# Modulation sums of a two-block transformer kernel: four row groups side by side on the partitions, and an opening in smaller steps

## What is computed

```python
    c_act = jax.nn.silu(c)                       # (1, 2048)
    for l in range(DEPTH):                       # DEPTH = 2
        shift, scale, gate = jnp.split(c_act @ w_ada[l] + b_ada[l], 3, axis=-1)   # w_ada[l]: 2048 x 6144
        h = rms_norm_2(x, norm_w[l]) * (1.0 + scale[:, None, :]) + shift[:, None, :]
        ...
        x = x + gate[:, None, :] * y
```

## Time and profile before

| | |
|---|---|
| median of three runs | 2554.61 us |
| profiled execution: span from the first to the last instruction | 2553.1 us |
| PE busy | 2513.7 us (98%) |
| DVE busy | 1935.9 us (76%) |
| ACT busy | 1223.6 us (48%) |
| DMA, mean over the span | 202 GB/s |

### The profile page before, as it was taken

One profiled execution on the slowest core, in us unless ns is written; L12 is line 12 of the kernel. 1 busy time (PEld: TensorE's weight loads), 2 busy tenths in 40 slices (PEclk: granted clock), 3 DMA queues, 4 the chain that ended last, 5 costly groups with the idle time before them and its releaser, 6 DMA issues.

```text
span 2553.1 us, 33576 instructions
## 1 busy us (share of the span) xinstructions
PE 2513.7 (98%) x12735; PEld 2109.3 (83%) x12735; DVE 1935.9 (76%) x3285; ACT 1223.6 (48%) x1808; POOL 15.1 (1%) x32
## 2 busy tenths in 40 slices
PE   8999999999999999999999999999999999999999
PEld 6888888888888888878888869888788798888777
DVE  7888988998899888676555647666986667668875
ACT  4444444444444444445555446453455565434553
POOL 0000000000000000000000000000000000000000
PEclk9999999999999999999999999999999999999999
DMA  8787777777787867545445445444445544444444
GB/s 307 257 294 268 277 255 284 280 272 273 247 292 267 299 228 279 202 162 185 142 136 177 157 116 179 150 141 138 143 158 182 176 150 150 134 133 157 153 161 139
DMA packets 266016, 516.95 MB, mean 202 GB/s; under 512 B 16576, under 2 KB 20992, under 8 KB 265216
## 3 DMA queue, kind: packets, MB, share of 16 engines
q1 hardware_dynamic: 264256, 508.43, 58.4%
q0 software_dynamic: 1600, 6.38, 1.0%
HBM read 512.68 MB, written 2.10 MB: 202 GB/s over the span
## 4 chain that ended last, share of the span: by engine, by line
PE 87%; DVE 8%; ACT 3%; issue 2%; DMA 0%; DVEq 0%; SPq 0%; ACTq 0%
PE proj L572 15%; PE proj L574 14%; PE proj L573 14%; PE proj L1223 7%; PE proj L1225 7%; PE proj L1224 7%; PE scores L702 3%; DVE w_lo L1836 2%; PE proj L1215 1%; PE proj L1217 1%; PE proj L1218 1%; PE proj L612 1%; DVE arena L1962 1%; PE proj L613 1%; PE proj L614 1%
## 5 line engine op out<-in xcount | busy, mean ns | idle before, releaser
L1836 DVE TENSOR_TENSOR w_lo<-w_raw,w_hi 128x1024 fp32r<-128x1024 f32 (+1 forms) x740 | 895.2, 1218 | 297.4 <-ACT w_hi L1264 238.7
L1264 ACT ACTIVATE w_hi<-w_raw 128x1024 fp32r<-128x1024 f32 (+1 forms) x740 | 772.9, 1052 | 625.1 <-PE proj L574 374.3
L572 PE MATMUL proj<-w_hi,xt_lo 128*128 128x512 f32 x1632 | 650.9, 399 | 4.1 <-DVE xt_lo L1850 4.0
L574 PE MATMUL proj<-w_hi,xt_hi 128*128 128x512 f32 x1632 | 637.8, 391 | 0.0
L573 PE MATMUL proj<-w_lo,xt_hi 128*128 128x512 f32 x1632 | 636.6, 390 | 0.0
L1223 PE MATMUL proj<-w_hi,xt_lo 128*128 128x512 f32 x976 | 395.5, 405 | 3.5 <-DVE w_lo L1836 3.5
L1225 PE MATMUL proj<-w_hi,xt_hi 128*128 128x512 f32 x976 | 380.9, 390 | 0.0
L1224 PE MATMUL proj<-w_lo,xt_hi 128*128 128x512 f32 x976 | 380.5, 390 | 0.0
L572 PEld LDWEIGHTS proj<-w_hi,xt_lo 128*128 128x128 f32 x1632 | 307.3, 188 | 67.1 <-DVE xt_lo L1850 5.7
L574 PEld LDWEIGHTS proj<-w_hi,xt_hi 128*128 128x128 f32 x1632 | 306.9, 188 | 65.5
L573 PEld LDWEIGHTS proj<-w_lo,xt_hi 128*128 128x128 f32 x1632 | 307.5, 188 | 60.3
(11 more groups left out here) (402 smaller groups left out, 2812.4 us busy)
## 6 DMA issues: line engine op xcount, KB each, us to landing
w_raw<-in_dsa_w_in_dram SPq DMA_DIRECT2D x159, 1024.0 KB, 7.3
w_raw<-in_w_in_dram SPq DMA_DIRECT2D x120, 1024.0 KB, 5.1
arena<-in_w_ada_dram SPq DMA_DIRECT2D x192, 512.0 KB, 5.9
w_raw<-in_w_out_dram SPq DMA_DIRECT2D x32, 1024.0 KB, 5.1
w_raw<-in_mla_w_in_dram SPq DMA_DIRECT2D x24, 1024.0 KB, 5.1
w_raw<-in_dsa_w_out_dram SPq DMA_DIRECT2D x16, 1024.0 KB, 5.1
w_raw<-in_mla_w_out_dram SPq DMA_DIRECT2D x16, 1024.0 KB, 5.1
w_raw<-in_mla_w_ukv_dram SPq DMA_DIRECT2D x8, 1024.0 KB, 5.6
```

Source lines behind the costliest of these rows:

```text
L572: mm(o, xt[1][:, k0 + kk, tok], WH[:, c % 2, k, 0:n], start=first, stop=False)
L574: ins = mm(o, xt[0][:, k0 + kk, tok], WH[:, c % 2, k, 0:n], start=False, stop=last)
L1264: A(hi[:, 2 * q:2 * q + 2, 0:n], RAW[:, c % 4, 2 * q:2 * q + 2, 0:n], ACT.Copy).then_inc(hi_made, 1)
L1836: V.tensor_tensor(lo[:, ks, 0:n], RAW[:, c % 4, ks, 0:n], hi[:, ks, 0:n].bitcast(F32), ALU.subtract).then_inc(lo_made, 1)
```

## The change

The change has two parts.

**Modulation sums.** The 192 pieces are cut in another way. Before, a piece was 256 rows of one layer by 512 columns. Now it is 32 rows of both layers by 2048 columns: the four column groups of 512 stand one above the other on the partitions (32 rows each), and each layer has its own transfer (256 KB) and its own accumulator of 512 columns. `c` is loaded four times, once for each group of 32 partitions, so that each partition finds its value. After 64 pieces, a third (shift, scale or gate) is complete in both layers, and PE adds up with a selector of four columns (`QUAD`, one for each group of 32 partitions) in place of the column of ones: each product then gives 4 x 128 results. There are 3 groups of 8 such products. Each layer has one accumulator only, so DVE waits for PE's products before it starts the next third.

**Opening.** The first quarter of `x` is loaded in two parts from ACT's queue, the first chunk's first half in two transfers, and the identity alone comes first. PE runs seven products of ones with ones before any data is there. Half 0 is built in two steps of one row group each, and its products are ordered high times high first. The second and fourth quarter of `x` are turned in the two PSUM banks of the attention, so they don't wait for the first. DVE makes the angles at `h == 2`, and `X_AT` is 1, 3, 5.

```diff
-ADA_COLS, ADA_K = 12, 8
-ADA_PIECES = DEPTH * ADA_COLS * ADA_K
+ADA_THIRDS, ADA_K = 3, 64
+ADA_PIECES = ADA_THIRDS * ADA_K
-X_AT = (0, 3, 6, 8)
+X_AT = (1, 3, 5)
+def ada_row(a):
+    s, j = a % ADA_K // 16, a % 16
+    return j * P + 32 * s
+    for n in range(4):
+        c[:, K_QUAD + n] = i // 32 == n
+        def bank_of(g, t):
+            return ((TP[0], TP[1]), (SP, PV))[g % 2][t]
 # SP: the pieces
-                        src = io["w_ada_2"][l][2 * k * P:2 * (k + 1) * P, b * BW:(b + 1) * BW]
-                        sp.dma_start(ARAW[:, a % 3], src.rearrange("(k p) n -> p k n", p=P)).then_inc(ada_loaded[a % 3], 16)
+                        for l in range(DEPTH):
+                            src = io["w_ada_2"][l, row:row + 32, e * D:(e + 1) * D].rearrange("r (g n) -> g r n", g=4)
+                            sp.dma_start(ARAW[:, a % 3, l, :], src).then_inc(ada_loaded[a % 3], 16)
 # SP: the opening
-            sp.dma_start(CST[:, 0:K_MASK], io["constants"][:, 0:K_MASK]).then_inc(ident_loaded, 16)
-            load_x(0)
+            sp.dma_start(IDENT, io["constants"][:, 0:K_INV]).then_inc(ident_loaded, 16)
             first = w[0:CK * P, 0:BW].rearrange("(k p) n -> p k n", p=P)
-            sp.dma_start(RAW[:, 0, 0:2], first[:, 0:2]).then_inc(first_half_loaded, 16)
+            sp.dma_start(RAW[:, 0, 0:1], first[:, 0:1]).then_inc(w_first, 16)
+            sp.dma_start(RAW[:, 0, 1:2], first[:, 1:2]).then_inc(first_half_loaded, 16)
...
+            sp.dma_start(CST[:, K_INV:K_MASK], io["constants"][:, K_INV:K_MASK]).then_inc(inv_loaded, 16)
             load(1, w, CK, 0)
-            sp.dma_start(small[:, 48:64], io["c_2"]).then_inc(S("c_loaded"), 16)
+            for g in range(4):
+                sp.dma_start(CR[32 * g:32 * g + 32, :].rearrange("r (s j) -> r s j", s=4),
+                             io["c_2"].rearrange("(s r) j -> r s j", s=4)).then_inc(S("c_loaded"), 16)
+            sp.dma_start(QUAD, io["constants"][:, K_QUAD:K_QUAD + 4]).then_inc(S("quad_loaded"), 16)
 # PE
+            def warm_up():
+                pe.wait_ge(warm, 1)
+                for _ in range(7):
+                    mm(PV[:, 0:P], ONES[:, :], ONES[:, :], start=True, stop=True)
+            def turn_first(part):
+                if part == 0:
+                    pe.wait_ge(ident_loaded, 16)
+                pe.wait_ge((x_first, x_loaded[0])[part], 16)
+                for t in range(T):
+                    for kt in (2 * part, 2 * part + 1):
+                        ins = nc.tensor.transpose(TP[t][:, kt * P:(kt + 1) * P], X[:, t, kt * P:(kt + 1) * P], IDENT)
+                ins.then_inc(turned, 1)
+            def first_half():
+                turn_first(0)
...
+                pe.wait_ge(turn_hi, 1)
+                pe.wait_ge(first_hi, 1)
+                for k in range(2):
+                    if k == 1:
+                        turn_first(1)
+                        pe.wait_ge(hi_made, 1)
+                    for t in range(T):
+                        mm(PJ[0][t][:, :], XTH[:, k, t * P:(t + 1) * P], WH[:, 0, k, :], start=k == 0, stop=False)
...
+                    for t in range(T):
+                        mm(PJ[0][t][:, :], XTL[:, k, t * P:(t + 1) * P], WH[:, 0, k, :], start=False, stop=False)
...
+                    for t in range(T):
+                        ins = mm(PJ[0][t][:, :], XTH[:, k, t * P:(t + 1) * P], WL[:, 0, k, :], start=False, stop=False)
+                ins.then_inc(half_used, 1)
 # PE: columns
-                for q in range(4):
-                    at = 384 + 48 * l + 4 * b + q
-                    ins = mm(SP[:, at:at + 1], ACC[:, e % 2, q * P:(q + 1) * P], ONES[:, 0:1], start=True, stop=True,
-                             skip_group_check=True)
+                for l in range(DEPTH):
+                    for q in range(4):
+                        at = 384 + 48 * l + 16 * e
+                        o = SP[:, at:at + 16].rearrange("p (g q) -> p g q", g=4)[:, :, q]
+                        ins = mm(o, ACC[:, l, q * P:(q + 1) * P], QUAD, start=True, stop=True,
+                                 skip_group_check=True)
 # ACT
+            act.dma_start(X[:, :, 0:256], x[:, :, 0:256]).then_inc(x_first, 16)
+            act.dma_start(X[:, :, 256:512], x[:, :, 256:512]).then_inc(x_loaded[0], 16)
+            def first_his():
+                act.wait_ge(w_first, 16)
+                A(WH[:, 0, 0, :], RAW[:, 0, 0, :], ACT.Copy).then_inc(first_hi, 1)
+                first_part(0)
+                act.wait_ge(first_half_loaded, 16)
+                A(WH[:, 0, 1, :], RAW[:, 0, 1, :], ACT.Copy).then_inc(hi_made, 1)
+                first_part(1)
 # DVE
+            V.memset(ONES[:, :], 1.0).then_inc(warm, 1)
+            def first_lows():
+                dve.wait_ge(first_hi, 1)
+                V.tensor_tensor(WL[:, 0, 0, :], RAW[:, 0, 0, :], WH[:, 0, 0, :].bitcast(F32), ALU.subtract).then_inc(first_lo, 1)
+                first_part_low(0)
+                dve.wait_ge(hi_made, 1)
+                V.tensor_tensor(WL[:, 0, 1, :], RAW[:, 0, 1, :], WH[:, 0, 1, :].bitcast(F32), ALU.subtract).then_inc(lo_made, 1)
+                first_part_low(1)
-                    if k0 == 0 and e > 1:
-                        dve.wait_ge(ada_columned, e - 1)
+                    if k == 0 and e > 0:
+                        dve.wait_ge(ada_columned, e)
+                    dve.wait_ge(ada_loaded[a % 3], 32 * (a // 3) + 32)
+                    for l in range(DEPTH):
+                        o, w, c = ACC[:, l, :], ARAW[:, a % 3, l, :], CR[:, k:k + 1]
...
-                if h == 1:
+                if h == 2:
                     angles()
                     sines()
```

More of the change, by code:

```diff
@@ L758, in summed @@
                     nonlocal ends
-                    while ends < DEPTH * ADA_COLS and ADA_AT[ADA_K * ends + ADA_K - 1] + 2 <= slot:
+                    while ends < ADA_THIRDS and ADA_AT[ADA_K * ends + ADA_K - 1] + 2 <= slot:
                         columns(ends, seen)
@@ L1372, in _ @@
                     act.sem_inc(sin_made, 1)
-                    act.wait_ge(S("c_loaded"), 16)
-                    A(small[:, 48:64], small[:, 48:64], ACT.Silu).then_inc(c_ready, 1)
+                    act.wait_ge(S("c_loaded"), 64)
+                    A(CR, CR, ACT.Silu).then_inc(c_ready, 1)
                 if h == 11:
```

106 lines of the change are left out of this document (69 added, 37 removed).

## The result

| | before | after |
|---|---|---|
| median of 4 runs | 2554.61 us (2554.49 to 2555.04) | 3207.85 us (3187.49 to 3215.22) |
| profiled execution, span | 2553.1 us | 3213.4 us, of 3215.22 us |
| granted clock, whole span | 0.999 | 0.930 |

The account below looks back on a forecast made before the run. The prediction took PE to bound the stretch of the sums, other engines hidden. Span 2553.1 - 14.6 (products) - 1.5 (waits) + 0.1 (opening) = 2537.1 us; the median, 1.5 us above, gives 2538.6 us, range 2533 to 2543.

Parts of the forecast that it names:

- The transfers of the sums: Loads of w_ada: 384 transfers of 256 KB instead of 192 of 512 KB still land in time, put at 0.
- the 15 that the prediction named as a sign of being wrong: Landing of w_ada: the prediction would be wrong if it passed 15 us, about what three buffers give.
- SP has room: SP's list: 192 more issues stand in front of the weight loads, which land after 7.3 us; put at 0.
- the transfers become the bound: Rival: smaller transfers of 32 rows land later than 15 us, delaying DVE and then PE; about 2700 us, chance 0.04.
- The modulation products: On PE: 24 products of 0.20 us, 4.9 us instead of 19.4, saving 14.6 us; two waits gone save 1.5 more.
- The sums on DVE: 384 operations of 512 columns instead of 768 of 256, each between 479 and 958 ns; hidden, put at 0.
- The new wait: DVE waits for PE's products at slots 109 and 213, 1.9 us each; covered by slack, 0, at most 3.8 us.
- The opening: Before about 40 us: half 2 starts earlier, but half 7 at 37.6 against 37.47; +0.1 us.
- the prediction's own upper bound of +2: In the opening: chunk 1 lands 1 us later and the chain is a further 1 us slower, +2 us.

Follow-up runs that it names:

- experiment 10: Separate program that only loads w_ada in seven phases of twelve 256 KB transfers, varying the source's outermost dimension, then copies x: 206.9 us in all.
- experiment 1: The whole change, with the source of each w_ada transfer having 32 rows outermost instead of four column groups: 2543.58 us, ratio 0.9949 to the kernel before.
- experiment 5: The kernel before, with each w_ada piece loaded by two 256 KB transfers of 128 rows in natural order: 2558.28 us, ratio 1.0009.
- Experiment 2: The kernel before with only the change's modulation sums, rows outermost in their transfers, and its own opening: 2538.25 us, ratio 0.9934.
- Experiment 3: The kernel before with only the change's opening and its own sums: 2558.03 us, ratio 1.0003.
- experiment 8: The whole change with 32 rows outermost, plus reordered opening: angles and their inputs earlier, ACT's sines and DVE's tables one half later: 2533.19 us, ratio 0.9912.
- experiment 4: The kernel before, each w_ada piece loaded by two 256 KB transfers, rows dealt to partitions so the source's outermost dimension is 4: 3191.13 us.
- Experiment 6: The kernel before, each w_ada piece loaded by two 256 KB transfers, rows dealt to partitions so the source's outermost dimension is 8: 2821.22 us.

## Why the prediction was wrong

**The transfers of the sums: the step that failed.** The prediction said "Even if two halves came one behind the other at 5.9 us each, 11.8 us is under 15", and put the transfers at 0. It took the landing of a 512 KB transfer as a bound for a 256 KB one, so it asked for the bytes alone. The diff ahead of it showed the shape too, `"r (g n) -> g r n"` with g = 4, and the prediction didn't work out what it does. In the chain of the changed kernel a transfer of the sums takes 15.8 us (above, at 1011.17), over the 15 that the prediction named as a sign of being wrong. The other half of the step, "SP has room", failed with it.

The rate follows from rows now. From 60 to 500 us the changed kernel issued 106 transfers of `w_ada` and 43 of weights. The four engines carried 106 x 0.262 = 27.8 MB of sums, 6.9 MB each, and each engine 43 x 1.049 / 16 = 2.8 MB of weights: 9.8 MB in 440 us, 22 GB/s. Alone an engine reached 25.5 (experiment 10), so these four were at 87% of that; an engine of the kernel before moved 276 / 16 / 0.78 = 22 GB/s while it was busy, so by that rate they were full. Both are estimates from those numbers. The others carried 2.8 MB. The share of 0.55 is more than four full engines and such a load on twelve give (4 + 12 x 2.8 / 9.8) / 16 = 0.46; what kept the others busy beyond it isn't shown. To keep the pace of experiment 1 (177 transfers of sums and 72 of weights in this window), each of the four would have had to carry 11.6 + 4.7 = 16.3 MB, that is 37 GB/s. At 25.5 GB/s 16.3 MB take 640 us, 1.45 times the 440; at the 22 GB/s that the four had, 1.67 times. The stretch of the sums is 1610 us against 959, 1.68 times as long. The 1.67 only restates the pace; the bound that doesn't rest on this kernel's own rate is the 1.45.

The Trainium skill states the rule: by "DMA: Bandwidth & Descriptors", section "Why a DMA increments its semaphore by 16 and not by 1", a transfer is given to the largest number of engines, at most 16, that divides the slowest dimension of both of its patterns, and its section "Rules for kernel authors" warns of an outermost dimension below 16. The trace agrees: shares of 0.24 and 0.13, rates of 102 and 51 GB/s, and the counts of small packets. The prediction had weighed another section of that page, on size, and experiment 5 shows that this one would have cost at most 0.2%.

The rival "the transfers become the bound" had the right chain (the pieces late, DVE behind them, PE behind DVE) and a price of about 2700 us, from a landing of 16 us. It had the wrong cause, the size, and a chance of 0.04. Its cost went by DVE's pieces alone; that SP is held at the issue (2.88 us each) and the weights come late behind it, 832.1 us of waiting on ACT, it didn't have.

**The clock.** While PE waits piece by piece, the granted clock in the windows is 0.85 to 0.87, between the two levels of 2.4 and 1.2 GHz; before it was 1.00. It is a consequence: in experiment 1, without those waits, it is 1.00 again. It makes PE's work longer, but PE was busy for 312 of 440 us and not the bound.

**The modulation products: right.** Forecast 24 x 0.20 = 4.9 us for the products and two waits gone, and with the opening's +0.1 a total of 2538.6. Experiment 2 has the sums alone: 2538.25 us. A group takes 1.71 us, forecast 1.6.

**The sums on DVE: right.** An operation of 512 columns takes 746 ns, between the bounds of 479 and 958 ns. DVE's busy time from 60 to 500 us is 382.75 us in experiment 1, against 394.73; DVE stays hidden there.

**The new wait: right in sign, wrong in length.** Forecast 1.9 us for each stop; it was 3.46 and 4.2 us in experiment 2. The term that was off is DVE's lead: it came to the wait 1.6 us before PE began the group (355.89 - 3.46 = 352.43, against 354.00), where 360.65 - 360.37 = 0.3 was taken. The cover was there, as said: PE waits 0.6 us in 950.

**The opening: right chain, mis-sized.** Forecast +0.1 us, from half 7 at 37.6. The changed kernel's PE in the opening, the starts of halves 1, 2, 3 and 4, two products of half 4, then halves 6 and 7, and the window of half 4's slow products:

```profile
13.95 0.47 PE L594 MATMUL proj<-w_hi,xt_lo 128*128 128x512 f32 x1 [0.76 <-DVE w_lo L1928]
...
16.75 0.39 PE L594 MATMUL proj<-w_hi,xt_lo 128*128 128x512 f32 x1
...
22.32 0.50 PE L594 MATMUL proj<-w_hi,xt_lo 128*128 128x512 f32 x1 [1.81 <-DVE w_lo L1928]
...
27.26 0.47 PE L594 MATMUL proj<-w_hi,xt_lo 128*128 128x512 f32 x1 [1.92 <-DVE w_lo L1928]
...
28.25 0.60 PE L595 MATMUL proj<-w_lo,xt_hi 128*128 128x512 f32 x1
28.64 0.63 PE L596 MATMUL proj<-w_hi,xt_hi 128*128 128x512 f32 x1
...
35.73 0.47 PE L594 MATMUL proj<-w_hi,xt_lo 128*128 128x512 f32 x1 [0.26 <-DVE w_lo L1928]
...
39.99 0.50 PE L594 MATMUL proj<-w_hi,xt_lo 128*128 128x512 f32 x1 [1.27 <-DVE w_lo L1928]
```

```profile
28.30:32.00 3.70, 3.70 (x13) 2.81 (x12) 0.00 (x0) 0.00 (x0) 0.00 (x0) 0.54 1.04 380
```

The waits stand where the prediction has them, in front of halves 3, 4, 6 and 7, all for `w_lo`. The starts were forecast at 15.6, 21.8, 26.2, 33.2 and 37.6 for halves 2, 3, 4, 6 and 7. Half 2 was 1.1 us later, because PE itself was at half 1 until then (13.95 + 2.8), which the chain left out. Half 4 brought the next delay: behind the waits of 1.81 and 1.92 us its products start 0.4 us apart (28.25, 28.64) where 0.23 is usual, as at the lower level of the clock; from 28.3 to 32.0 us the granted clock is 0.54. It takes 4.4 us, from 27.26 to 31.63, instead of 2.85. Half 7 comes at 39.99 us, 2.5 later than before, beyond the prediction's own upper bound of +2. Experiment 3 has the same delay in the opening alone, and experiment 8 shows that the order makes it: with the angles, ACT's sines, the tables and the first transfers in another order, no product after 11 us runs at the lower level, half 7 starts at 32.99, and the time is 2533.19 us. Which of these moves brought how much wasn't tried. That is 5 us below experiment 2, by medians from different groups of runs (ratios 0.9912 and 0.9934, intervals that overlap a little), and half 7's lead over the earlier trace rows is 4.5 us.

Experiment 1 lies 5.3 us above experiment 2; their profiled spans lie 3.5 us apart (2539.8 and 2536.3), of which the opening explains 2.7 (half 7 at 39.98 and 37.26) and PE's waits for `w_lo` between 60 and 1010 us (1.2 against 0.6) another 0.6. The rest is within the spread of the runs.

**Open.** Why dealing single rows in turn to the engines costs time even with all 16 at work isn't settled: the runs show the price (14.37 against 11.86 us alone, 57 us in the kernel) and not the mechanism. At four outermost it has no part that shows (34.13 and 33.98 us alone, and experiment 4 is no slower than the changed kernel, which deals no rows). Experiment 6 stays open: alone, eight engines reach the full 25 GB/s each with dealt rows, but in the kernel it took 160 us more than the 2660 that was the most expected.

## What to carry to other kernels

Before a transfer's size, look at the order of its dimensions: here the source's outermost dimension decided how many of the 16 DMA engines carried it, and with 4 outermost 3.1 MB took 34 us instead of 12.6. A mean DMA share well under 1 isn't proof of room: when landings are late and the issues themselves get long (2.88 us here, 0.60 with the rows outermost), look whether a few engines carry everything. When a step of an opening is brought forward, what stood behind it comes in front of something else: list for each engine in order what the next engine waits for, and put everything else behind it.

## What the runs showed of the hardware that was not expected

- One DMA engine moved 25 to 25.5 GB/s of these rows (51, 102, 201 GB/s with 2, 4, 8 outermost).
- The number of packets under 512 B fits one for each engine and transfer (824 in experiment 10, 384 x 12 between the changed kernel and experiment 1), so a page alone can tell that transfers run on few engines.
- Transfers on four engines hold up those that all 16 carry: the 1 MB weight loads behind them in the queue landed after 16.1 us instead of 7.3 (experiment 1: 8.3).
- With sixteen outermost the DMA share rose to 1.01 while the rate fell from 276 to 257 GB/s, so a share of 1 doesn't mean the highest rate.
- Transfers of 256 KB in a steady stream cost no measurable time against 512 KB (ratio 1.0009 [0.9999, 1.0019]).
- After two waits of just under 2 us, with 2.9 us of work between them, PE's products ran at the lower level from about 1 us after the second (granted clock 0.54 from 28.3 to 32.0 us; half 4 takes 4.4 us in experiments 1 and 3, too); after waits of 0.37 to 1.01 us (experiment 8) they didn't.
